# One core, RWKV-7 time mixing: the inversion of the diagonal blocks on VectorE instead of GpSimd

## The reference

```
def step(s, inp):
    w_t, k_t, v_t, kk_t, a_t = inp[:5]
    sa = jnp.einsum('bhvk,bhk->bhv', s, kk_t)
    s = (s * w_t[:, :, None, :]
         - sa[..., None] * (kk_t * a_t)[:, :, None, :]
         + v_t[..., None] * k_t[:, :, None, :])
    y = jnp.einsum('bhvk,bhk->bhv', s, inp[5]) if len(inp) > 5 else None
    return s, y
```

## Time and profile before

| | us |
|---|---|
| median of 3 runs | 6022.49 (6011.25 to 6033.48) |
| profiled execution | 6034.74 |
| its span | 6032.9 |
| TensorE matmul, busy in the span | 5347.0 (89%) |
| VectorE, busy | 2652.4 (44%) |
| ScalarE, busy | 1745.9 (29%) |
| GpSimd, busy | 1280.9 (21%) |

### The profile page before, as it was taken

The page is one execution under the profiler, slowest core; times in us unless marked ns, Lnnn a source line. Parts: engine busy times, 40 slices in busy tenths (PEclk is TensorE's granted clock), DMA queues, the critical chain, the costliest instruction groups (busy, mean ns, idle before and its releaser), DMA issues. The chain is left out here.

```text
span 6032.9 us, 146336 instructions
## 1 busy us (share of the span) xinstructions
PE 5347.0 (89%) x56750; PEld 3287.6 (54%) x56750; DVE 2652.4 (44%) x4658; ACT 1745.9 (29%) x4007; POOL 1280.9 (21%) x2745
## 2 busy tenths in 40 slices
PE   6999997999999879999999986887888888888879
PEld 1666662333333235444444436777777777777734
DVE  0333435666666422222232224444544444554466
ACT  0222112443334303221122113333333333333322
POOL 0011102222222100000000003333333343344333
PEclk9999998999999989999999998999999999999989
DMA  6122211000000253221111213333433333333275
GB/s 247 56 66 67 64 56 41 21 21 22 21 21 22 113 206 139 74 72 52 63 63 60 68 59 87 89 89 86 96 89 87 87 89 93 94 88 91 66 241 181
DMA packets 774962, 504.36 MB, mean 84 GB/s; under 512 B 509248, under 2 KB 726976, under 8 KB 767296
## 3 DMA queue, kind: packets, MB, share of 16 engines
q1 hardware_dynamic: 774336, 495.75, 28.5%
HBM read 312.10 MB, written 183.50 MB: 82 GB/s over the span
## 5 line engine op out<-in xcount | busy, mean ns | idle before, releaser
L1534 PE MATMUL p_bU<-keep_hT,p_slab 128*128 128x512 f32 (+1 forms) x2592 | 1029.3, 559 | 12.8 <-DMA p_slab<-in_o_w_in_dram 7.3
L1534 PEld LDWEIGHTS p_bU<-keep_hT,p_slab 128*128 128x128 f32 x2592 | 493.1, 191 | 543.8 <-issue 512.3
L883 PE MATMUL at_bS<-at_qT,at_kT 97*64 97x512 f32 (+1 forms) x2368 | 601.6, 598 | 8.5 <-issue 7.9
L1015 DVE TENSOR_REDUCE at_mx<-at_bM 128x1 f32<-128x512 f32 (+1 forms) x656 | 400.5, 629 | 354.9 <-PE at_bM L849 351.9
L978 ACT ACTIVATE at_pT<-at_bS 128x512 f32<-128x512 f32 (+1 forms) x592 | 346.8, 591 | 462.8 <-PE at_bS L883 385.9
L2345 DVE SCALAR_TENSOR_TENSOR rw_S<-rw_bank,rw_dec,rw_Sdec 128x64 f32<-128x64 f32 x576 | 137.0, 279 | 768.5 <-PE rw_bank L2100 768.5
L1606 DVE SCALAR_TENSOR_TENSOR p_z<-p_u,p_shift,p_z 128x2306 f32<-128x2306 f32 x26 | 68.2, 2621 | 769.9 <-ACT p_z L1564 769.9
L2000 PE MATMUL rw_bank<-keep_ident,rw_XB 64*64 64x64 f32 x2304 | 128.4, 264 | 236.6 <-DMA rw_XB<-scratch_inverses 231.7
L1909 POOL TENSOR_TENSOR rw_g_at<-rw_g_at,rw_g_prod 64x14 f32<-64x14 f32 (+6 forms) x1008 | 316.7, 314 | 79.0
L1907 POOL TENSOR_TENSOR rw_g_prod<-rw_g_at 64x14 f32<-64x14 f32 (+6 forms) x1008 | 310.6, 308 | 79.4
L883 PEld LDWEIGHTS at_bS<-at_qT,at_kT 97*64 97x64 f32 x2368 | 160.5, 137 | 267.3 <-issue 215.0
(11 more groups left out here) (266 smaller groups left out, 10068.4 us busy)
## 6 DMA issues: line engine op xcount, KB each, us to landing
rw_zin<-scratch_heads SPq DMA_DIRECT2D x144, 512.0 KB, 4.9
mod_w<-in_ada_w_dram SPq DMA_DIRECT2D x4, 6144.0 KB, 18.3
scratch_heads<-p_z SPq DMA_DIRECT2D x24, 1024.0 KB, 4.9
rw_lin<-scratch_lora SPq DMA_DIRECT2D x144, 128.0 KB, 5.4
scratch_bv<-rw_bv SPq DMA_DIRECT2D x144, 128.0 KB, 1.8
scratch_products<-rw_NB SPq DMA_DIRECT2D x288, 64.0 KB, 2.5
rw_XB<-scratch_inverses SPq DMA_DIRECT2D x288, 64.0 KB, 4.3
scratch_y<-rw_ysb SPq DMA_DIRECT2D x288, 64.0 KB, 2.1
```

What stands on the lines that cost most here:

```text
L883: last = pe.matmul(bS[rows, g % 3, 0:nq * P], kT[:, s, k * P + VH * x:k * P + VH * x + VH], qT[:, s, q0 * P:(q0 + nq) * P], start=True, st ...
L1015: nc.vector.tensor_reduce(mx[:, j, piece:piece + 1], bM[:, (FIRST_ITEM[b] + i) % 2, 0:n], AX.X, ALU.max).then_inc(max_red, 1)
L1534: last = pe.matmul(bU[:, n % 4, 0:w], slab[:, i, k, :], hT[:, k, tok:tok + w], start=(k == 0), stop=(k == KD - 1))
```

## The change

GpSimd's list loses `invert`; VectorE's list gets it, one body later, behind `parameters` and ahead of `carry(n, 0)`. It inverts index n+1 in body n, where GpSimd inverted index n+2 in body n. GpSimd keeps `before`. SyncE's list, its waits and all DMAs stay as they are, and so do the lists of TensorE and ScalarE. The two copies out no longer have a wait between them. Two small waits vanish: GpSimd's on its own `before`, and the one behind the last copy.

```diff
             @block.gpsimd
...
                 def body(n, has):
                     if has[3]:
                         before(n.on(3))
-                    if has[2]:
-                        invert(n.on(2), has[3])
...
+                def invert(m):
+
+                    half = BLOCKS
+                    STEPS = 2 * (SUB - 2)
+                    link = Link(v, inv_chain, (STEPS + 2) * m.n)
+                    N = g_at[:].rearrange("p (i j) -> p i j", j=SUB)
+                    v.wait_ge(g_l, 16 * 2 * (m.n + 1))
+                    settle(v, settled[3])
+                    link(nc.vector.tensor_copy(g_at[0:half, :], g_in[0:half, ::-1]))
+                    settle(v, settled[3])
+                    link(nc.vector.memset(g_at[:, ::SUB + 1], 1.0))
+                    for k in range(1, SUB - 1):
+                        rows = SUB - 1 - k
+                        prod = g_prod[:, 0:rows * k].rearrange("p (i j) -> p i j", j=k)
+                        below = N[:, k + 1:, 0:k]
+                        link(nc.vector.tensor_tensor(prod, N[:, k + 1:, k:k + 1].broadcast_to([2 * half, rows, k]),
+                                                     N[:, k:k + 1, 0:k].broadcast_to([2 * half, rows, k]), ALU.mult))
+                        link(nc.vector.tensor_tensor(below, below, prod, ALU.add))
+                    if m.since(1):
+                        v.wait_ge(i_st, 16 * m.n)
+                    settle(v, settled[3])
+                    nc.vector.tensor_copy(g_out[0:half, :], g_at[0:half, ::-1]).then_inc(inv_done, 1)
+                    nc.vector.tensor_copy(g_out[half:, :], g_at[half:, :]).then_inc(inv_done, 1)
...
                     if has[3]:
                         parameters(l)
+                    if has[1]:
+                        invert(m)
                     if has[0]:
                         carry(n, 0)
                         decayed(n, 1)
```

More of the change, by code:

```diff
@@ L1883, in _ @@
             def _(g):
-                STEPS = 2 * (SUB - 2)
                 def before(m):
@@ L1889, in before @@
                     nc.gpsimd.tensor_tensor(cx[:], cs[:], ee[:, 0], ALU.subtract).then_inc(cx_done, 1)
[L1891 to L1917, removed]
                 nc.gpsimd.memset(zeros[:], 0.0).then_inc(zero_set, 1)
```

## The result

The changed kernel takes 6341.79 us (median of 4 runs, 6336.86 to 6356.34) against 6024.88 us before: the ratio is 1.053, with a 95% interval of 1.0513 to 1.0546. It is slower by 317 us; forecast were 6392 and a range of 6290 to 6495.

What follows compares the result with a forecast made beforehand. It took the ring through SyncE and GpSimd's inversion as the bound; the new road 10.5 + 4.6 + 6.5 + 12.6 = 34.2 us against 28.88, over 70 bodies +371, together +369, gives 6392 us, range 6290 to 6495.

Steps and rivals of the forecast that it cites:

- The ring store, loads, products, gather, GpSimd: RWKV stage before the change: SyncE's cycle through GpSimd's 12.66 us inversion sets the period, 28.34 us in one body.
- The start of the inversion and its place: VectorE's list: the inversion starts 2.27 us behind TensorE's head, with its blocks already there.
- The price of the chain: Inversion on VectorE: 28 steps 0.24 us apart make 6.7 us, with copies and memset 8.1 us.
- (a): VectorE's steps cheaper: inversion of 5 us, period 31.2 us, +165 us, 6187 us; chance 0.08.
- Behind the store: SyncE and TensorE after the inverses' store at +10.5: 4.6 us to loads, 6.5 to TensorE's start, 12.6 to next head.
- The wait for `carry`: TensorE's state step 1: new wait of some 3.4 us plus perhaps 1.7 of clock loss, hidden by 3.6 us.
- GpSimd's interference: VectorE's operations slowed by GpSimd: 0.1 to 0.2 us a body goes away, counted as nothing; at most 14 us.
- (b): VectorE's steps much dearer, 0.35 us apart: inversion 11.2 us, period 37.3, +590 us; chance 0.08.
- (c): Not slower: inversion at most 2.9 us, store at +5.34 or earlier; at 2.6 us the kernel takes 6001; chance 0.02.

Runs made afterwards that it cites:

- the second chain on VectorE: The kernel before plus an unread second inversion of zeros on VectorE at the change's place, GpSimd's inversion kept: 6034.01 us, ratio 1.0026.
- Half of the inversion: The changed kernel with only the first 7 of the 14 elimination steps: 6119.78 us, ratio 1.0159.
- The version with all three: The changed kernel with inversion ahead of VectorE's bonus product, inverses' store and loads first in SyncE's list, inputs' loads behind the gather: 5869.04 us, ratio 0.9753.

## Why the prediction was right

**What bounds the kernel.** Right. The ring store, loads, products, gather, GpSimd bound it before; it is shortened by 1.5 us a body when the inputs' loads leave it, and lengthened again by 0.6 when the bonus stores enter it.

**The start of the inversion and its place.** Right. VectorE's chain starts behind the head without a wait for the gather, at +2.07 in the body shown, 0.2 earlier than reckoned from the earlier trace rows: the first copy starts 0.07 behind the parameters' copy, not behind its end. GpSimd at the same place shows that the place costs, and the second chain on VectorE shows that its 8 us of work do not.

**The price of the chain.** 8.1 forecast, 7.95 measured. The groups by form (mean ns of one after the busy us) confirm the size of a step, at 0.98 ns an element from 14 to 56 where 1.16 were taken from the earlier trace rows:

```profile
L2341 DVE TENSOR_TENSOR rw_g_at<-rw_g_at,rw_g_prod 64x56 f32<-64x56 f32 x136 | 28.3, 208 | 4.7
...
L2339 DVE TENSOR_TENSOR rw_g_prod<-rw_g_at 64x14 f32<-64x14 f32 x137 | 22.8, 167 | 4.7
```

The two copies out were too dear: together 0.59, the second 0.31 behind the first, where 0.80 were taken. The copy in with its gap (0.47) and the 28 steps with the gap behind them (6.79 for 6.7) were near their terms. At 14 elements a product takes 0.167 us and at 56 elements 0.208. For these, estimates by the 58 cycles of rival (a), from VectorE: DVE Perf Modes of the Trainium skill, section on the TRN2 errata, are 0.075 and 0.119 us, which the trace refutes. The same section of the Trainium skill says that this row under-predicts a single operation. By the 151 cycles that it gives as measured for a tensor_tensor of 512 and 2048 elements the estimates are 0.172 and 0.216, within 4% of the trace.

**Behind the store.** The largest error of the sum: 10.11 for 10.5 on the store, and 10.72 for 11.1 from there to TensorE's start, together 0.8 us a body; the rest of the body was 0.17 longer than taken. By 70 bodies this is 42 of the 50 us between 6392 and 6341.79. Why the landing is 0.3 sooner was not tried by itself; the case with no inputs ahead of it shows what such a distance hangs on.

**The wait for `carry`.** It is there and it is hidden, as forecast, 2.4 us in place of 3.4. The clock loss behind it was taken too large: 1.7 us in every body. In the body shown there is none, the granted clock is 1.00 from 4640.7 to 4645.5, behind a wait of 1.56. Six bodies later it is there in full:

```profile
4843.14 0.45 PE L2024 MATMUL rw_bank<-rw_S,rw_AR 64*64 64x64 f32 x8 [2.65 <-DVE rw_S L2313]
...
4853.86 1.02 PE L1968 MATMUL rw_bank<-keep_ident,rw_XB 64*64 64x64 f32 x16 [4.41 <-DMA rw_XB<-scratch_inverses]
```

```profile
4843.10:4847.90 4.80, 4.76 (x80) 4.79 (x82) 3.38 (x6) 1.23 (x4) 1.27 (x1) 0.64 0.65 162
```

Of the 68 bodies, 45 have a granted clock of 1.00 in the 4.8 us behind this wait and TensorE needs 4.90 from there to the inverses; 23 have 0.64 on average and need 6.40, 1.5 us more. Over all bodies that is 0.5 us in place of 1.7. TensorE is therefore at the inverses by +16.0 on average, not +18.0, and the wait for them is 4.8, not 3.6. Behind this second wait the clock is lower: 0.50 from 4651.1 to 4656.0 in the body shown, behind 4.62 (0.65 in the earlier trace rows, behind 2.82), and 0.61 over 4.9 us on average (0.72 in the kernel before). This stretch is on the road. It is in the rest of the body, 12.77 where 12.6 were taken and where the kernel before has 12.42; with the second chain on VectorE, where this clock is 0.97, the rest takes 11.52. As the wait for the inverses takes up whatever TensorE gains ahead of it, the mistake about `carry` moved no time.

**GpSimd's interference.** VectorE's L2292, the counterpart of L2324 in the earlier trace rows, now takes:

```profile
L2292 DVE TENSOR_TENSOR rw_Bc<-rw_b,rw_en 128x512 f32<-128x512 f32 x70 | 48.0, 685 | 0.0
```

0.085 us less. It was counted as nothing and could not be seen in the time.

**Rivals.** (a) and (b) fall with the steps, which are 0.20 to 0.24 apart. No run puts (c) to the test as it stands, with the store back at +5.34. Half of the inversion is on the side of its condition: with the store at +6.82 the kernel is still 1.6% slower than before. The version with all three is faster with the store at +5.89, where the way from the store to TensorE's start is 8.63 in place of 11.12. Two sums of the rivals are off: (c)'s chain of 2.6 has the copies at 0.07 apart as well, and with the 1.35 that the prediction gives for copies and memset it is 3.3, over the 2.9 that (c) needs; and 2.3 by 70 in (a) is 162, not 165. Neither changes the forecast.

## What to carry to other kernels

When work moves from a slow engine to a fast one, sum the road from the event that lets the new engine begin, not from the one that let the old one begin: here 4.7 us less work came 4.8 us later. Load on an engine costs little as long as the delay it makes hides behind another wait (0.3% for 8 of 29 us here); a delay on the road of the period costs nearly in full (3.04 of 3.29 us, and 1.38 of 1.38), and what sets it here is the place of an item in an in-order list, SyncE's list of DMAs too. Before such a move, list every item that shares a queue with the moved one, and try the queue's order first: it gave 1.7% by itself, and with the list and the place right the move went from a loss of 5.3% to a part, 43 us, of a gain of 2.5%. With only the inputs' loads moved, it was still a loss of 206 us against the kernel before with the same edit.

## What the runs showed of the hardware that was not expected

- The four 64 KB loads of the inverses land in 4.0 to 4.3 us (medians of the changed kernel and of the one before) behind 1.3 MB of inputs on the same queue, and in 2.3 to 2.6 where the inputs are not ahead of them. Where no inputs' loads stand between the store of the inverses and the loads that wait for its landing, these came 2.65 us behind the store in the body shown, 3.17 on average.
- In the changed kernel waits of 0.7 to 3.4 us for `carry` are followed by a granted clock of 1.00 in 45 bodies and of 0.64 on average in 23 (4.8 us behind the wait; the two levels are 1.2 and 2.4 GHz). The length alone does not decide: the wait of 1.90 before 4057.94 has 0.64 behind it and the one of 3.44 before 5118.47 has 1.00. Where it is low, TensorE needs 6.40 us to the inverses in place of 4.90.
- A chain of 28 operations of 14 to 56 elements on VectorE, each waiting for the one before through a semaphore whose threshold comes from a register, costs 0.20 to 0.24 us a step, where the operations themselves take 0.17 to 0.21. Without a wait between them, two copies of 4 elements start 0.07 us apart, though each is 0.16 long.
